# A one-layer hybrid decoder step: where the sample attention stands among the expert steps, a front with other queues and turns, and a tail by quarters

## What is computed

```
n = rmsnorm(x)
h = x + W_out[ rms(attention(n)) ; rms(short_conv(n)) ]        # one input projection W_in for all
h = h + PEER(rmsnorm(h))                                       # per token: 8 heads x 16 experts,
        sum over experts of softmax(g) * gelu(n . u_tab[e]) * v_tab[e]
y = h + sigmoid(rmsnorm(h) W_g) * (p W_p)
```

## Time and profile before

| | us |
|---|---|
| median of 3 runs | 2547.03 |
| lowest, highest | 2544.01, 2556.1 |
| profiled execution, its own time | 2548.46 |
| its span | 2546.6 |
| mean granted TensorE clock | 0.784 of 2.4 GHz |

### The profile page before, as it was taken

One profiled execution on the slowest core, in us unless ns is written; L12 is line 12 of the kernel. 1 busy time (PEld: TensorE's weight loads), 2 busy tenths in 40 slices (PEclk: granted clock), 3 DMA queues, 4 the chain that ended last, 5 costly groups with the idle time before them and its releaser, 6 DMA issues.

```text
span 2546.6 us, 21559 instructions
## 1 busy us (share of the span) xinstructions
PE 1701.0 (67%) x8372; PEld 921.9 (36%) x8372; DVE 1151.5 (45%) x2141; ACT 334.1 (13%) x731; POOL 915.6 (36%) x644
## 2 busy tenths in 40 slices
PE   7999998998987668788787333323233333577677
PEld 3445675696775347433475000000000000122224
DVE  2010213124455763544533666566665665544342
ACT  1000232010001322200100101101011002001002
POOL 0000000013223453422433565656666555555430
PEclk9998996998998776599698666666666565787788
DMA  8953373779999998999998999999999999999996
GB/s 316 351 180 114 114 291 112 269 245 412 388 377 379 362 382 311 394 390 385 415 410 338 420 418 421 421 421 421 422 421 422 421 421 417 399 416 416 416 418 224
DMA packets 215845, 908.75 MB, mean 357 GB/s; under 512 B 17351, under 2 KB 40880, under 8 KB 131809
## 3 DMA queue, kind: packets, MB, share of 16 engines
q0 software_dynamic: 92160, 671.13, 63.9%
q1 hardware_dynamic: 123368, 235.41, 26.1%
q10 hardware_dynamic: 216, 0.86, 0.1%
HBM read 895.31 MB, written 14.53 MB: 357 GB/s over the span
## 4 chain that ended last, share of the span: by engine, by line
DMA 46%; PE 39%; DVE 6%; issue 3%; POOL 3%; ACT 3%; SPq 0%; DVEq 0%; PEldq 0%; ACTq 0%; POOLq 0%
DMA arena<-in_peer_v,arena 19%; DMA arena<-in_peer_u,arena 15%; PE bank L1725 9%; DMA arena<-in_w_in 5%; PE bank L2175 4%; PE bank L2160 4%; DVE arena L1521 3%; DMA arena<-in_w_out 3%; PE bank L1799 2%; DMA arena<-in_peer_wq 2%; PE bank L1936 2%; PE bank L1912 2%; PE bank L2109 2%; DMA arena<-in_state_win 2%; PE bank L2284 2%
## 5 line engine op out<-in xcount | busy, mean ns | idle before, releaser
L1521 DVE CUSTOM_DVE_ANT_0 arena<-arena 128x2048 f32<-128x2048 f32 x320 | 730.8, 2292 | 581.2 <-DMA arena<-in_peer_u,arena 577.9
L2160 PE MATMUL bank<-arena 128*32 128x512 f32 x2560 | 463.4, 828 | 670.8 <-DVE arena L1530 523.7
L675 POOL DMA_INDIRECT arena<-in_peer_u,arena x320 | 566.2, 1769 | 862.1 <-DVEq L1500 577.1
L680 POOL DMA_INDIRECT arena<-in_peer_v,arena x320 | 349.1, 1091 | 691.0 <-PE bank L2160 663.7
L2160 PEld LDWEIGHTS bank<-arena 128*32 128x32 f32 x2560 | 68.8, 127 | 1004.5 <-DVE arena L1530 508.4
L1725 PE MATMUL bank<-arena 128*128 128x512 f32 (+2 forms) x544 | 217.0, 559 | 5.3 <-PE bank L1725 2.6
L2175 PE MATMUL bank<-arena 128*128 128x192 f32 x1024 | 188.2, 346 | 25.6 <-DMA arena<-in_w_in 24.1
L2175 PEld LDWEIGHTS bank<-arena 128*128 128x128 f32 x1024 | 179.7, 203 | 46.9 <-DMA arena<-in_w_in 31.3
L1725 PEld LDWEIGHTS bank<-arena 128*128 128x128 f32 (+1 forms) x544 | 101.4, 208 | 117.2 <-issue 116.8
L987 ACT ACTIVATE arena<-arena 128x4 f32<-128x4 f32 x80 | 16.8, 211 | 864.1 <-DVE arena L1521 863.9
L2284 PE MATMUL bank<-arena 128*128 128x512 f32 x256 | 124.8, 647 | 0.0
(11 more groups left out here) (267 smaller groups left out, 1519.9 us busy)
## 6 DMA issues: line engine op xcount, KB each, us to landing
arena<-in_w_in SPq DMA_DIRECT2D x22, 2048.0 KB, 9.2
arena<-in_w_in SPq DMA_DIRECT2D x32, 1024.0 KB, 16.1
arena<-in_w_out SPq DMA_DIRECT2D x8, 2048.0 KB, 9.8
arena<-in_peer_wq SPq DMA_DIRECT2D x8, 2048.0 KB, 8.3
arena<-in_w_out SPq DMA_DIRECT2D x16, 1024.0 KB
arena<-in_peer_wq SPq DMA_DIRECT2D x16, 1024.0 KB
arena<-in_ple_gate SPq DMA_DIRECT2D x32, 512.0 KB, 14.4
arena<-in_ple_gate SPq DMA_DIRECT2D x6, 2048.0 KB, 12.2
```

The source lines that it names most:

```text
L675: pool.indirect_dma_start(u_row[j], None, I["peer_u"][0], bass.IndirectOffsetOnAxis(idx[:, i, c + j:c + j + 1], 0)).then_inc(u_in[j], 16)
L680: pool.indirect_dma_start(v_row[j], None, I["peer_v"][0], bass.IndirectOffsetOnAxis(idx[:, i, c + j:c + j + 1], 0)).then_inc(v_in[j], 16)
L1521: dve.tensor_tensor_reduce(out=u_row[j], in0=u_row[j], in1=rep_of(i), scale=1.0, scalar=0.0, op0=ALU.mult, op1=ALU.add, accum_out=a4[:, pa ...
L2160: ins = pe.matmul(bank[i % 2][32 * q:32 * q + 32, :], diag[:, k % 2, j, :], v_row[j][:, 512 * q:512 * q + 512], start=(s == 0 and j == 0), ...
```

## The change

It has four parts.
- The front. The nine gain loads and the bias table are issued by ACT and no longer by SP, so that SP begins with the constants and x; the second block of W_in is requested ahead of the other x tiles. The first 16 turns of x go to four banks and are evacuated four at a time by DVE. `raw_out` is shared between DVE (even ones) and ACT (odd ones). In the eight prompt heads of the first tile, `turn_probs(u)` goes ahead of `scores(u + 2)` and `head_sums(u - 1)` ahead of `values(u)`.
- The expert steps. On TensorE, `sample_scores(k - 11)` stands behind rows(k) in steps 11 to 14, and `sample_values(k - 13)` behind rows(k) in steps 13 to 15; they were ahead of rows(k). On ACT their parts stand behind gelu(k) in the same way. DVE's order does not change.
- The last prompt gate block. Two of its four last quarters go ahead of rows(78), its sigmoid and multiplication into step 79, ahead of gelu(79) and of the weighing; the four sample products with W_p go to steps 76 and 79 and to banks of their own.
- The tail. The last accumulator is added, turned and multiplied by quarters of 512 channels; y of the fourth prompt block is written ahead of the last gate weights.

```diff
-        for i, name in enumerate(("norm1", "norm2", "norm3", "out_gain")):
-            sp.dma_start(gain_rows[KC * i:KC * i + KC, :], I[name][0].rearrange("(k p) -> k p", p=128)).then_inc(gains_in, 16)
-        for w in range(3):
-            sp.dma_start(gain_rows[64 + 8 * w:72 + 8 * w, :], I["conv_w"][0, w].rearrange("(c p) -> c p", p=128)).then_inc(gains_in, 16)
-        sp.dma_start(gain_rows[88:96, :], I["conv_b"][0].rearrange("(c p) -> c p", p=128)).then_inc(gains_in, 16)
-        sp.dma_start(gain_rows[96:97, :], I["qk_gain"][0, 0:1, :]).then_inc(gains_in, 16)
-        sp.dma_start(tab[0:NBUCKET, :], I["rel_bias"]).then_inc(first_in, 16)
...
         fill_z(0)
+        fill_z(1)
         sp.dma_start(h[:, 1, :], xp[1]).then_inc(x_in, 16)
         sp.dma_start(h[0:64, 2, :], xs).then_inc(x_in, 16)
         sp.dma_start(h[64:128, 2, :], xs).then_inc(x_in, 16)
-        fill_z(1)
...
+        ple_load(4)
+        ple_load(5)
...
-            if i == 1:
-                ple_load(4)
-                ple_load(5)
-        y_out(3)
+            if i == 2:
+                y_out(3)
...
+        for i, name in enumerate(("norm1", "norm2", "norm3", "out_gain")):
+            act.dma_start(gain_rows[KC * i:KC * i + KC, :], I[name][0].rearrange("(k p) -> k p", p=128)).then_inc(gains_in, 16)
+        for w in range(3):
+            act.dma_start(gain_rows[64 + 8 * w:72 + 8 * w, :], I["conv_w"][0, w].rearrange("(c p) -> c p", p=128)).then_inc(gains_in, 16)
+        act.dma_start(gain_rows[88:96, :], I["conv_b"][0].rearrange("(c p) -> c p", p=128)).then_inc(gains_in, 16)
+        act.dma_start(gain_rows[96:97, :], I["qk_gain"][0, 0:1, :]).then_inc(gains_in, 16)
+        act.dma_start(tab[0:NBUCKET, :], I["rel_bias"]).then_inc(first_in, 16)
...
-            for c in range(NB + 2):
+            for c in range(1, NB + 2, 2):
                 act.wait_ge(t_mm, tcount[0] + c + 1)
-                src = bank[6 + c % 2]
+                src = bank[7]
...
-            if items and k != 16:
+            if items and not 13 <= k < 17:
...
-            if i in (6, 9, 12):
+            if i in (6, 9, 12, 15):
                 gate_sigmoid((i - 6) // 3)
             gelu(k)
+            if 13 <= k < 16:
+                before_gelu(items[0])
+            if 11 <= k < 15:
+                sample_keys(k - 11)
...
-        even_transposes(KC, lambda e, c: e.tensor_scalar(xT[:, c, 0:128], bank[6][:, 0:128], gT[:, 0, c:c + 1], None, ALU.mult))
+        for c in range(0, KC, 4):
+            dve.wait_ge(turn_mm, c // 4 + 2)
+            dve.tensor_tensor(xT[:, c:c + 4, 0:128], bank[4 + c // 4][:, :].rearrange("p (c t) -> p c t", c=4),
+                              rep(gT[:, 0, c:c + 1], [1, 4], [0, 128]), ALU.mult).then_inc(turn_ev, 1)
...
+        dve.wait_ge(xn_ready, 1)
+        raw_out(0)
...
-                 6: lambda: prompt_y(0), 9: lambda: prompt_y(1), 12: lambda: prompt_y(2)}
+                 6: lambda: prompt_y(0), 9: lambda: prompt_y(1), 12: lambda: prompt_y(2), 15: lambda: prompt_y(3)}
...
+        def last_turned(q):
+
+            dve.wait_ge(hT_mm, 2 + q + 1)
+            dve.tensor_tensor(hT_s[:, 4 * q:4 * q + 4, :], bank[6 + q % 2][:, 0:256].rearrange("p (c t) -> p c t", c=4),
+                              rep(gT[:, 2, 4 * q:4 * q + 1], [1, 4], [0, 64]), ALU.mult).then_inc(hT_ev, 1)
+
+        for q in range(4):
+            dve.wait_ge(acc_ev, SUBS + q)
+            v = h[32:64, 2, 512 * q:512 * q + 512]
+            dve.tensor_tensor(v, acc[32:64, 512 * q:512 * q + 512], v, ALU.add).then_inc(h_seen, 1)
+            if q:
+                last_turned(q - 1)
+        last_turned(3)
...
-        transposes(KC, tok_tiles(x_tile, (0,)))
-        pe.wait_ge(t_ev[0], 8)
-        pe.wait_ge(t_ev[1], 8)
+        for c in range(KC):
+            ins = pe.transpose(bank[4 + c // 4][:, 128 * (c % 4):128 * (c % 4) + 128], x_tile(0, c), ident)
+            if c % 4 == 3:
+                ins.then_inc(turn_mm, 1)
+        pe.wait_ge(turn_ev, 5)
...
+            turn_probs(u)
             if u < NH - 2:
                 scores(u + 2)
-            turn_probs(u)
-            values(u)
             if u:
                 head_sums(u - 1)
+            values(u)
...
-            for v in items[0:0 if k == 16 else 1]:
+            for v in items[0:0 if 13 <= k < 17 else 1]:
                 item(v)
             weighted_rows(k)
+            if 13 <= k < 16:
+                item(items[0])
+            if 11 <= k < 15:
+                sample_scores(k - 11)
...
+            if i == 2 * SSTEP - 1:
+                pe.wait_ge(sig_ready, 4)
+                sample_ple(2)
+                sample_ple(3)
+            if i == 2 * SSTEP - 2:
+                prompt_gate(28)
+                prompt_gate(29)
             weighted_rows(LAST + i)
...
+                if blk == 3:
+                    sample_ple(0)
+                    sample_ple(1)
...
+        def last_turn(q):
+
+            pe.wait_ge(h_seen, SUBS + q)
+            if q >= 2:
+                pe.wait_ge(hT_ev, 4 + q - 1)
+            for c in range(4 * q, 4 * q + 4):
+                ins = pe.transpose(bank[6 + q % 2][:, 64 * (c % 4):64 * (c % 4) + 64], h[0:64, 2, 128 * c:128 * c + 128],
+                                   ident[0:64, 0:64])
+            ins.then_inc(hT_mm, 1)
+
+        def first_gate(q):
+
+            pe.wait_ge(hT_ev, 4 + q + 1)
+            for c in range(4 * q, 4 * q + 4):
+                ins = sample_gate(0, c, gate_w[gate_slot(24 + c // 2)][:, c % 2, :], c == 0, c == KC - 1)
+            return ins
...
+        last_turn(0)
+        last_turn(1)
+        first_gate(0)
+        last_turn(2)
+        first_gate(1)
+        last_turn(3)
+        first_gate(2)
+        ins = first_gate(3)
```

More of the change, by code:

```diff
@@ L337, in build @@
     LAST_COLS = (3, 2, 0, 1)
+    PLE_BANK = (2, 3, 4, 5)
     def gate_slot(q):
@@ L1101, in _ @@
                 pick_exp(8 + s // 4)
-        gate_sigmoid(3)
-        odd_transposes(KC, lambda e, c: e.activation(hT_s[:, c, :], bank[7][:, 0:64], ACT.Copy, scale=gT[:, 2, c:c + 1]))
         root(stats[:, 146:147], stats[:, 149:150])
@@ L1193, in _, with raw_out @@
         ins.then_inc(xn_ready, 1)
+        def raw_out(kind):
+            even_transposes(NB + 2, lambda e, c: e.tensor_copy(
+                raw[kind][:, :, 2 * c:2 * c + 2, :].rearrange("p m s c -> p s c m"),
+                bank[6][:, :].rearrange("p (s c m) -> p s c m", s=2, m=STRIDE)))
+        dve.wait_ge(xn_ready, 1)
+        raw_out(0)
         dve.wait_ge(small_in, 16 * 2)
@@ L1678, in _ @@
             s = sig[0:64, blk % 2, :]
-            step(dve.tensor_tensor(s, s, bank[4 + blk % 2][0:64, :], ALU.mult))
-            dve.sem_inc(ple_mm, 1)
+            step(dve.tensor_tensor(s, s, bank[PLE_BANK[blk]][0:64, :], ALU.mult))
             v = h[0:64, 2, 512 * LAST_COLS[blk]:512 * LAST_COLS[blk] + 512]
@@ L1756, in _ @@
         blocks(2, 6, 1)
-        pe.wait_ge(t_ev[0], 16)
-        pe.wait_ge(t_ev[1], 16)
+        pe.wait_ge(t_ev[0], 8)
+        pe.wait_ge(t_ev[1], 8)
         pe.wait_ge(bias_sb, 1)
@@ L2253, in _, with sample_ple, prompt_gate @@
                 ins.then_inc(pleT_mm, 1)
+        def sample_ple(i):
+            slot = LAST_COLS[i] % 2
+            if i >= 2:
+                pe.wait_ge(ple_in[slot], 16 * 3)
+            for c in range(2):
+                ins = pe.matmul(bank[PLE_BANK[i]][0:64, :], pleT[:, c, 256:TOK], ple_w[slot][:, c, :],
+                                start=(c == 0), stop=(c == 1))
+            ins.then_inc(ple_used, 1)
+        def prompt_gate(q):
+            blk, part = divmod(q, 8)
+            if part == 0:
+                if blk == 0:
+                    pe.wait_ge(hT_ev, 4)
+                else:
+                    pe.wait_ge(y_ready, blk)
+                pe.wait_ge(ple_in[blk % 2], 16 * (blk // 2 + 1))
+                for t in range(2):
+                    for c in range(2):
+                        ins = pe.matmul(bank[6 + t][:, :], pleT[:, c, 128 * t:128 * t + 128], ple_w[blk % 2][:, c, :],
+                                        start=(c == 0), stop=(c == 1))
+                ins.then_inc(ple_used, 1)
+                if blk == 3:
+                    sample_ple(0)
+                    sample_ple(1)
+            pe.wait_ge(gw_in[gate_slot(q)], 16 * (q // GW + 1 if q < 29 else 1))
+            for t in range(2):
+                for k in range(2):
+                    ins = pe.matmul(bank[4 + t][:, :], hT[:, 2 * part + k, 128 * t:128 * t + 128], gate_w[gate_slot(q)][:, k, :],
+                                    start=(part == 0 and k == 0), stop=(part == 7 and k == 1))
+            ins.then_inc(gw_used, 1)
+            if part == 7:
+                pe.wait_ge(gw_used, q + 1)
+                pe.sem_inc(gate_mm, 1)
         pe.wait_ge(pleT_ev, 1)
         for i in range(2 * SSTEP):
+            if i == 2 * SSTEP - 1:
[5 more added lines that the diff above has]
+                prompt_gate(29)
             weighted_rows(LAST + i)
```

(17 more changed lines are left out.)

73 lines of the change are left out of this document (18 added, 55 removed).

## The result

The changed kernel takes 2566.8 us (median of 9 runs, 2563.5 to 2569.3) against 2549.1 us for the kernel before (9 runs, 2543.8 to 2556.1): a ratio of 1.0067, 95% interval 1.0055 to 1.0080, slower by 17 us. The prediction was 2570 us, range 2537 to 2586. The profiled execution took 2569.3 us with a span of 2567.5, 20.9 more than before's span.

A forecast was written before the change was run, and what follows sets the result against it. Chain 46% transfers, 39% TensorE; in steps 12 to 14 not bandwidth but engine hand-overs. 2548.46 - 9.3 (front) - 16 (tail) + 49 (steps) = 2572, less 1.4 for the profiled run: about 2570 us, range 2537 to 2586.

The forecast's parts named there:

- Start of the front: Kernel start: x loaded earlier and its 16 turns faster, first product near 13.7 us, 7 us earlier (5 to 8).
- Raw rows: Raw-row evacuations shared by DVE and ACT: first kind 1.1 us earlier, second 1.2, together 2.3 us gained (0 to 5).
- The hand-over of two banks: Second kind of raw rows: turns and hand-over of two banks limit it, gain taken as 1.2 us.
- Heads: Prompt heads: scores fill TensorE's 0.83 us wait per head, at most 6.6 us over eight; nothing taken.
- Steps: Steps 11 to 16: rows, values, scores, DVE's softmax, dots, diag become one chain, 178.8 against 129.6 us, 49 lost.
- Key load of pair 2: Steps 13 to 14: requested 18 us later, lands at 989.7, wanted at 991; just fits, nothing added.
- the two readings: Key load's 34 us: either constant, 1 us from late, or caused by sharing with gather rows, shrinking when gathers pause.
- Tail: Behind the last gather: work moved into step 79 and done by quarters, 16 us gained (12 to 18).
- the floor: Tail: last 12.6 MB of weights take until 2518, so the end is no earlier than 2527 to 2530.
- 1 (value tiles earlier): Expert steps: value-tile requests set the pace, change closes DMA gaps, 11 us gained, total 2511 us; chance 0.15.
- 2 (the clock): Expert steps: higher TensorE clock shortens rows and values, 20 us lost, total 2542; chance 0.22, including losses of 15 to 38.
- 3 (late loads): Expert steps: key or value loads late on top, from 8 us for one, total 2578 us or more; chance 0.08.

The follow-up runs named there:

- experiment 8: Changed kernel with the order of the expert steps and the order within the prompt heads both put back: 2525.9 us, ratio 0.9909 to the kernel before.
- experiment 2: Kernel before with only the order of the expert steps changed, front and tail as before: 2604.8 us, ratio 1.0194.
- experiment 5: Changed kernel with VectorE's maxima and weights of a pair's scores one step later, ScalarE's exponentials behind the gelu also in step 12: 2542.5 us, ratio 0.9953.
- experiment 3: Changed kernel with values ahead of the rows again, scores still behind the rows in steps 11 to 14: 2539.6 us, ratio 0.9940.
- 9: Kernel of experiment 1 with only step 15's values moved behind the rows (on ScalarE behind the gelu): 2524.5 us, ratio 0.9906 to the kernel before.
- 4: Kernel of experiment 3 with ScalarE's exponentials of a pair moved behind its gelu: 2537.8 us, ratio 0.9958 to the kernel before.
- experiment 1: Changed kernel with only the order of the expert steps put back, front and tail kept: 2528.4 us, ratio 0.9887; run again 2522.1 us, 0.9892.

## Why the prediction was right, step by step

- **Start of the front, 7 (5 to 8) forecast:** 6.4 at the first product and 5.6 at the last projection's end (271.2 against 276.8), within the range. Shown by the traces.
- **Raw rows, 1.1 + 1.2 forecast:** 2.7 for the first kind (9.7 us from the last projection to L1823, 12.4 before): besides the earlier start, a pair of tiles took 1.78 us there in place of 2.25. For the second, 15.9 against 15.3, and 15.0 in eight of the kernels above: 0.3 at best. There a pair of tiles took 1.78 us with two engines and had taken 1.8 with one (321.87 to 323.65 in before's timeline). Before, ScalarE made nine copies there back to back in 8.16 us; after, each copy takes 1.02 to 1.10 and each engine waits 0.75 us for TensorE ahead of it. The hand-over of two banks, which I had named as the limit, left no gain; the 1.2 was mis-sized, and the 1.1 too small. The sum, 2.1, is near the 2.3.
- **Heads, nothing forecast:** at most 2 us (experiment 8).
- **Steps, 49 forecast:** 48.2 and, alone, 49 with an interval of 40 to 59 (experiment 2). By stretch 29.0, 29.0, 45.0, 41.7, 34.1 forecast, 27.5, 29.7, 46.5, 40.8, 33.4 measured. In 13 to 14 the pieces were: rows 6.0 (5.5 forecast), values 14.1 (14.9), scores 10.7 (8.6), VectorE 5.9 (6.1), dots, diag and the hand-over to the rows 9.8 (9.9). The forecast took the scores of pair 3 for every pair. In the changed kernel the scores of the four pairs took 7.5, 7.4, 10.7 and 8.6 us, and the trace before had pair 2's 10.8 already, from 971.49 to 982.28 in its chain:

```profile
971.49 3.78 PE bank L2000 x16
...
982.28 3.45 PE bank L2160 x29
```

  VectorE's part was 4.7 and 7.0 us in the first two stretches, where 5 had been taken for both. The stretches missed by -1.5, 0.7, 1.5, -0.9 and -0.7: the mechanism was right, and that the sum came within 1 us is in part luck. That VectorE's wait for scores is a link is shown (experiment 5), and that the values' place is one too (3, 9). Each time some 21 us fewer came back in experiments 3, 4 and 5 than I had expected. In 3 and 4 that is mostly TensorE's own row, and 2.5 us a step that gelu, and so diag, stood behind ScalarE's copy of the values; in 5 it is late loads and ScalarE's copies for dots(16).
- **Key load of pair 2, "just fits":** it did not come near. Its last transfer was issued at 944.15, and the DMA view (KB, us to landing) has it in 10.2 us later, at 954.4; TensorE took the keys at 981.3:

```profile
arena<-in_state_win SPq DMA_DIRECT2D x1, 512.0 KB, 10.2
```

  The same load beside running gathers took 33.83 us in experiment 5. So it was not a constant of the load. Of the two readings in the prediction the trace agrees with that of the Trainium skill ("DMA: Bandwidth & Descriptors", "Queues, rings and completion order": each DMA engine serves the rings that have work in turn): the load was early once the gathers paused. From 944 to 954.4 they held 52.1% of the engines' time, against the 83.7% of the kernel before further down.
- **Tail, 16 (12 to 18) forecast:** 18.1 in the trace, just past the range; 13 (8 to 18) timed alone. The first block ended 14.0 us behind the last landing (14.8 forecast), and the later ones came every 7.4 us, with at most 0.3 us of idle time ahead of each. So the weights did not hold TensorE up. Yet the floor was well placed: the last weights, requested behind 2545, took 11.2 us, and the prediction's 2518 for them, 39 us later, is 2557. The end, 18.1 ahead of 2546.6, is 2528.5, inside the floor's 2527 to 2530.
- **Rivals:** 1 (value tiles earlier) has no support: the DMA share fell, and dots(14) started 37 us behind diag(13), far beyond the 6. 2 (the clock) neither: rows took 4.9 to 6.0 us and values 14 to 15, at a granted clock of 0.60 to 0.75, where it needed 3.6 and 8.4. 3 (late loads) did not occur in the changed kernel, but did once its gaps were closed (experiment 5).

## What to carry to other kernels

Before work is moved behind an instruction that another engine waits for, write down the whole round that leads back to the same instruction, through every engine; if the moved work lies on it, its full length is added to each step that it is in, however idle the engines look. Then add up each engine's own row for the same step as well, for the longer of the two sets the pace: experiments 3 and 4 failed by that. Count the in-order engine that only copies too: in experiment 3 a 0.2 us gelu stood behind a copy that waited 14.3 us for products, VectorE waited up to 9.3 us for that gelu, and 2.5 us of it reached TensorE. A small load whose request or whose cover moves is a third thing to look at (experiment 5). And where a change has parts that gain and one that loses, time them apart: here the parts without the new order give 0.989, the whole 1.007.

## What the runs showed of the hardware

The loads of past keys and values, in pieces of about 1 KB on SP's queue, are slow beside gathers and fast without. The queue rows of the DMA view, for 937 to 971 in the kernel before, then for 963 to 970 in experiment 1 (packets, MB, share of the 16 engines):

```profile
q0 software_dynamic: 1621, 11.71, 83.7%
q1 hardware_dynamic: 1757, 1.67, 14.7%
```

```profile
q1 hardware_dynamic: 1045, 1.00, 44.4%
```

That is 1.67 MB in 34 us or 49 GB/s, and 1.00 MB in 7 us or 143 GB/s. In the 34 us the two queues moved 1621 and 1757 of what the trace counts as packets, nearly one for one, though the gathers' are 7.2 KB on average and the loads' 950 bytes. A pair needs 1 MB of keys and 1 MB of values (four transfers of 128 KB and one of 512 KB each), so beside gathers some 43 us, an estimate from the 49 GB/s. With the order put back (experiment 1) TensorE waits for these loads in steps 11 and 12:

```profile
922.10 3.47 PE L2022 MATMUL bank<-arena 128*128 128x128 f32 x16 [16.28 <-DMA arena<-in_state_win]
945.19 0.69 PE L2052 MATMUL bank<-arena 128*128 128x128 f32 x2 [11.34 <-DMA arena<-in_state_win]
```

In the changed kernel its trace names no such wait: the scores stand later behind the request, and from step 13 on the chain stops the gathers. With it 11 to 13 is 7 us shorter there than before (57.2 against 64.5). Whether larger pieces or earlier requests would shorten the 38 to 41 us that 12 to 13 takes with the order put back was not tried and stays open.
